# Transfers asked for beside other work in a two-block transformer kernel: stages without computation removed, tables ahead of the zeros, the residual one tile behind the sums

## The reference, cut to what matters

```python
def first_block(x, c, ctx, ...):          # two layers; layer 0 also keeps the context
    for l in range(DEPTH):
        mod = silu(c) @ w_mod[l] + b_mod[l]              # shift, scale, gate, twice
        h = x * (1 + scale) + shift
        y = mixer_ab(h) if l == 0 else mixer_na(h)       # attention (+ Fourier mixing)
        x = layer_norm(alpha * x + gate * y, ln1)        # ln1 stage
        h = x * (1 + scale) + shift                      # h2 rows, stored to DRAM
        m = moe_ffn(h)                                   # 64 experts, top 8, one shared
        x = layer_norm(alpha * x + gate * m, ln2)        # combine stage

def fourier_mix(f, w_fnet):
    fr = fft2(f over tokens and 64 channels).real        # as products with tables
    return einsum("blgc,gcd->blgd", fr, w_fnet)

def second_block(x, ...):
    for i in range(DEPTH):
        h = h + 0.5 * rms_norm(swiglu(rms_norm(h)))      # ffn
        h = h + rms_norm(mixer(rms_norm(h)))             # conv + state space, or dilated attention
        h = h + 0.5 * rms_norm(swiglu(rms_norm(h)))      # ffn
```

## Time and profile before

| | |
|---|---|
| median of 3 runs | 3317.04 us (3316.82 to 3324.07) |
| profiled execution, its own time | 3318.03 us |
| its span, first to last instruction | 3316.2 us |
| TensorE busy / VectorE / ScalarE / GpSimd | 80% / 36% / 25% / 7% of the span |
| mean granted TensorE clock | 0.893 of full |
| TensorE weight loads | 56% of the span |
| moved | 810.85 MB, 245 GB/s over the span |

### The profile page before, as it was taken

One profiled execution on the slowest core, in us unless ns is written; L12 is line 12 of the kernel. 1 busy time (PEld: TensorE's weight loads), 2 busy tenths in 40 slices (PEclk: granted clock), 3 DMA queues, 4 the chain that ended last, 5 costly groups with the idle time before them and its releaser, 6 DMA issues. The chain is left out here.

```text
span 3316.2 us, 44216 instructions
## 1 busy us (share of the span) xinstructions
PE 2650.5 (80%) x17438; PEld 1848.6 (56%) x17438; DVE 1184.3 (36%) x1841; ACT 844.0 (25%) x1237; POOL 238.3 (7%) x210
## 2 busy tenths in 40 slices
PE   5777499999997598597744537999678979989699
PEld 4656444333342475343222217987437979987598
DVE  2433442211113535311110035449515445345344
ACT  2132111111111323111100004326314344334433
POOL 0000200121004010101100020000000000000000
PEclk8888689999998799699887768999798989989899
DMA  6373679999998323799999954423044434332451
GB/s 255 162 288 146 270 309 424 412 373 411 426 370 321 124 87 145 288 400 424 410 411 425 408 209 177 176 91 143 2 190 178 177 140 190 152 137 77 175 206 70
DMA packets 120122, 810.85 MB, mean 245 GB/s; under 512 B 31752, under 2 KB 33416, under 8 KB 67848
## 3 DMA queue, kind: packets, MB, share of 16 engines
q1 hardware_dynamic: 86264, 718.88, 54.0%
q0 software_dynamic: 19168, 53.65, 4.2%
q10 hardware_dynamic: 14512, 35.89, 2.8%
HBM read 762.12 MB, written 56.84 MB: 247 GB/s over the span
## 5 line engine op out<-in xcount | busy, mean ns | idle before, releaser
L2378 PE MATMUL psum<-second_x_hi,ffn_up_hi 128*128 128x256 f32 x1408 | 402.1, 286 | 45.4 <-DVE ffn_up_lo L2453 45.4
L2378 PE MATMUL psum<-second_x_lo,ffn_up_hi 128*128 128x256 f32 x1408 | 401.5, 285 | 0.0
L2378 PE MATMUL psum<-second_x_hi,ffn_up_lo 128*128 128x256 f32 x1408 | 401.3, 285 | 0.0
L1576 PE MATMUL psum<-experts_ahead_ring_up,moe_cols 128*64 128x512 f32 x1568 | 359.0, 611 | 35.4 <-issue 35.3
L2378 PEld LDWEIGHTS psum<-second_x_hi,ffn_up_hi 128*128 128x128 f32 x1408 | 273.6, 194 | 48.3 <-DVE ffn_up_lo L2453 46.9
L1940 DVE TENSOR_TENSOR experts_gated<-experts_silu,psum 128x256 f32<-128x256 f32 (+1 forms) x93 | 34.0, 366 | 679.7 <-ACT experts_silu L1726 679.7
L2378 PEld LDWEIGHTS psum<-second_x_lo,ffn_up_hi 128*128 128x128 f32 x1408 | 273.5, 194 | 1.4
L2378 PEld LDWEIGHTS psum<-second_x_hi,ffn_up_lo 128*128 128x128 f32 x1408 | 273.4, 194 | 0.0
L1583 PE MATMUL psum<-experts_ahead_ring_up,moe_cols 128*32 128x256 f32 x2432 | 170.6, 443 | 115.6 <-issue 115.6
L1576 PEld LDWEIGHTS psum<-experts_ahead_ring_up,moe_cols 128*64 128x64 f32 x1568 | 114.7, 141 | 245.4 <-issue 244.6
L2453 DVE TENSOR_TENSOR ffn_up_lo<-second_ring_up,ffn_up_hi 128x4096 fp32r<-128x4096 f32 x44 | 194.4, 4425 | 121.2 <-ACT ffn_up_hi L2415 121.2
(11 more groups left out here) (509 smaller groups left out, 4396.5 us busy)
## 6 DMA issues: line engine op xcount, KB each, us to landing
experts_ahead_ring_up<-in_experts SPq DMA_DIRECT2D x130, 2048.0 KB, 25.4
experts_ahead_ring_down<-in_experts SPq DMA_DIRECT2D x130, 1024.0 KB, 23.0
second_ring_up<-in_ffn SPq DMA_DIRECT2D x44, 2048.0 KB, 9.2
second_ring_down<-in_ffn SPq DMA_DIRECT2D x44, 1024.0 KB, 5.0
results<-experts_y ACTq DMA_DIRECT2D x49, 512.0 KB
second_ring_up<-in_attn_w_qkv SPq DMA_DIRECT2D x9, 2048.0 KB, 7.7
results<-ab_att_zeros SPq DMA_DIRECT2D x32, 512.0 KB, 13.6
ab_ahead_ab_in_w<-in_w_mod SPq DMA_DIRECT2D x6, 2048.0 KB, 16.0
```

Of the source, the lines that this page charges most:

```text
L1576: last = nc.tensor.matmul(psum[64 * e:64 * e + 64, bank, :], x[:, k, 64 * e:64 * e + 64], w[:, k, :, :].rearrange("p a n -> p (a n)"), sta ...
L2378: last = nc.tensor.matmul(psum[:, 2 * m + kind, 0:LAT], w[:, j, k, at], h[:, k, :], start=k == 0 and which == 0, stop=k == KD - 1 and whic ...
```

## The change

- `transpose_stage` and `rms_stage` take a function of SP's requests, run beside the stage's work. The requests of `ab_out` and of the first norm vectors go beside `qk_t`, those of `RouterInputs` beside `h2_cols`, the second block's first weights beside `first_rms`, with the small gain tables now ahead of them.
- The four first experts' weights are asked for at the start of `experts_stage`, by pairs: up, up, down, down.
- The Fourier tables have tiles of their own from before the attention stage on (class `Fourier`). They are asked for at the start of the attention stage, with the wait until they have landed, and then the zeros. The wait for the zeros goes into the third Fourier stage.
- Layer 1's modulation has a fourth buffer (the keys' tile, free by then), so its fourth chunk is asked for beside the turning `na_o`; VectorE runs `beside.dve` after its second tile's factors, ahead of the gains.
- Combine: four pairs of banks instead of two, so TensorE does not wait for `added`; SP asks for the vectors when the second gather has landed, gates first; VectorE's residual of tile t comes after the sums of tile t+1.

```diff
@@ class Modulation
+        if last is not None:
+            self.slots.append(last)
         self.depth = len(self.slots)
@@ class Vectors
-    def loads(self, sp):
-        for i, v in enumerate(self.vectors):
+    def loads(self, sp, gates_first=False):
+        order = list(range(len(self.vectors)))
+        for i in order[2:] + order[:2] if gates_first else order:
@@ def residual_norm_stage
-                beside.more_loads(sp)
+                if next_loads is None:
+                    beside.more_loads(sp)
                 beside.store(sp)
...
+                if step == 1 and next_loads is not None:
+                    beside.dve(dve)
                 if step >= 2:
...
-            if beside is not None:
+            if beside is not None and next_loads is None:
                 beside.dve(dve)
@@ def attention_stage
                 if idle_fill is not None:
                     sp.wait_ge(cleared, 1)
-                    fills = idle_fill.shape[0] // P
-                    for b in range(fills):
-                        sp.dma_start(idle_fill[b * P:(b + 1) * P, :], zeros[:]).then_inc(filled, 16)
-                    sp.wait_ge(filled, 16 * fills)
+                    for b in range(idle.shape[0] // P):
+                        sp.dma_start(idle[b * P:(b + 1) * P, :], zeros[:]).then_inc(filled, 16)
@@ class Fourier
+    def loads(self, sp):
+        sp.dma_start(self.tok[:], self.dft_tokens).then_inc(self.loaded, 16)
+        sp.dma_start(self.chan[:], self.dft_channels).then_inc(self.loaded, 16)
+        sp.wait_ge(self.cleared, 1)
+        for g in range(4):
+
+            at = slice((g % 2) * 64, (g % 2) * 64 + 64)
+            sp.dma_start(self.mix[at, g // 2, at], self.w_fnet[g]).then_inc(self.loaded, 16)
+        sp.wait_ge(self.loaded, 96)
@@ def fourier_stages, third stage
+            @block.sync
+            def _(sp):
+                zeros_there(sp)
@@ class ExpertRing
-        with nc.Block() as block:
-            @block.sync
-            def _(sp):
-                for item in range(KEPT):
-                    self.load_up(sp, item, self.place(item))
-                    self.load_down(sp, item, self.place(item))
+    def kept_loads(self, sp):
+        for pair in range(KEPT // 2):
+            for item in (2 * pair, 2 * pair + 1):
+                self.load_up(sp, item, self.place(item))
+            for item in (2 * pair, 2 * pair + 1):
+                self.load_down(sp, item, self.place(item))
@@ def experts_stage
+            ring.kept_loads(sp)
             sp.wait_ge(order_known, 1)
@@ def combine_norm_stage
-            sp.wait_ge(gathered[TOP_K - 1], 16)
-            vectors.loads(sp)
+            sp.wait_ge(gathered[1], 16)
+            vectors.loads(sp, gates_first=True)
...
-                if t >= 2:
-                    pe.wait_ge(added, (t - 2) * (TOP_K - by_pe) + 1)
...
-            for t in range(n):
-                sums(t)
-                if t >= 1:
-                    factors(t - 1)
-                residual(t)
-                if t >= 1:
-                    gain(t - 1)
+            for step in range(n + 1):
+                if step < n:
+                    sums(step)
+                if step >= 2:
+                    factors(step - 2)
+                if step >= 1:
+                    residual(step - 1)
+                if step >= 2:
+                    gain(step - 2)
             factors(n - 1)
             gain(n - 1)
@@ def first_block
                 transpose_stage(nc, f"h2_cols{layer}", psum, ident, KD, tok_tiles, lambda j, t: acc[:, t, j * P:(j + 1) * P],
-                                lambda engine, j, bank: copy_on(nc, engine, cols[:, j, 0:tok_tiles * P], bank[:, 0:tok_tiles * P]))
+                                lambda engine, j, bank: copy_on(nc, engine, cols[:, j, 0:tok_tiles * P], bank[:, 0:tok_tiles * P]), inputs.loads)
...
-                vectors.start()
+
+                def qk_loads(sp):
+                    for c in range(out_stream.depth):
+                        out_stream.load(sp, c)
+                    vectors.loads(sp)
+
+                zeros, filled = st.sbuf("zeros", [P, D]), st.sem("filled")
+                fourier = Fourier(nc, st, i["ab_w_fnet"], i["dft_tokens"], i["dft_channels"])
...
-                part = modulation(st, "mod_rest2", 1, 8, 4, 1, later=stream.wbuf, later_free=True)
+                part = modulation(st, "mod_rest2", 1, 8, 4, 1, later=stream.wbuf, later_free=True, last=k[:].rearrange("p c n -> p (c n)"))
@@ def second_block
-                part_loads(0)(sp)
-                sp.dma_start(gains[:], i["norm_g_cols"]).then_inc(loaded, 16)
-                sp.dma_start(ssm_gain[:], i["ssm_norm_g_cols"]).then_inc(loaded, 16)
-                sp.wait_ge(loaded, 32)
-        rms_stage(nc, "first_rms", x, acc, D, 2, x[:, 2, :])
+        def first_loads(sp):
+            sp.dma_start(gains[:], i["norm_g_cols"]).then_inc(loaded, 16)
+            sp.dma_start(ssm_gain[:], i["ssm_norm_g_cols"]).then_inc(loaded, 16)
+            part_loads(0)(sp)
+            sp.wait_ge(loaded, 32)
+
+        rms_stage(nc, "first_rms", x, acc, D, 2, x[:, 2, :], loads=first_loads)
```

108 lines of the change are left out of this document (53 added, 55 removed).

## The result

The changed kernel runs in 3290.39 us (median of 4 runs, 3289.31 to 3291.27) against 3320.19 us (4 runs, the three shown and one more): a ratio of 0.991, with a 95% interval of 0.9893 to 0.9927. It is faster, but by half of what was forecast (3256, range 3247 to 3267). The profiled execution takes 3289.31 us, its span is 3287.1, 29.1 us less than before.

The account below looks back on a forecast made before the run. Each stage ends with its slowest engine, so stretches where the computing engines idle (request blocks, three transfer waits) are time of the span. The terms sum to 61.0 us off 3318.0, giving 3257.0, stated as 3256; range 3247 to 3267.

Parts of the forecast that it names:

- Ahead of the attention: Output weights' requests beside the turning before the attention, which starts at 169.0 instead of 172.59: 3.6 us won.
- the first line of the table: Stretch from the start to the first attention product: 3.6 us forecast, 4.6 us won.
- Zeros and tables: Attention's end to first Fourier product: fills 3.7 us later, SP ends the stage, 11.3 us won, bounds 6 to 12.2.
- The rule on the latency of HBM under load: Wait for the Fourier tables: up to 2 us later by the skill page, total 3258; the sum did without it.
- SP holds the attention stage: Rival: tables land 5 us later, fills after them, Fourier start slips as much: 3261 to 3264; chance 0.12.
- The clock: First 13 Fourier products: after a pause of 1 to 2 us, full clock, 1.8 us won, between 0 and 1.9.
- Combine, layer 0 and layer 1: VectorE's gate-vector wait replaced by a shorter one for the second tile: 1.8 us (-3 to 5) and 3.0 (0 to 5).
- Norm, layer 1: VectorE's 6.28 us wait for vectors read back mostly gone through a fourth buffer: 5.7 us won, bounds 4 to 6.3.
- Layer 0's and layer 1's router and weights: Table requests beside the turning, router earlier: 8.7 us won in layer 0, 6.8 in layer 1 (bounds 0.5 to 8.4).
- the expert layers hide it: Rival: gathers wait for all weights, 2 to 4 us more in layer 0, nothing left in layer 1: 3265; chance 0.14.
- The seam: Between the blocks: norm starts beside the weight requests, nothing waits for weights, 18.3 us won, bounds 14 to 18.5.
- The rest of the span: Stretch from the first split of ffn weights to the end, untouched by the change: 0 us forecast.

Follow-up runs that it names:

- the restored blocks: Changed kernel with the two blocks of requests ahead of the turning restored in both expert layers: 3303.36 us, ratio 0.9947 to the kernel before.
- its repeat: The changed kernel itself run once more, unaltered, in another group of runs: 3294.43 us, ratio 0.9927 to the kernel before.
- the old stage in the changed kernel: Changed kernel with the combine stage of before (VectorE's order, requests' place and order, two pairs of banks): 3284.79 us, ratio 0.9873.
- first and third groups: Variants of the changed kernel and its repeat, beside the kernel before on one chip per group (3323.24 and 3321.04 us): 3277.77 to 3303.36 us.
- second group: Kernel before (3308.57 us) with new combine alone, 3329.16, or seam alone, 3293.71; changed kernel with wait behind fills, late vectors, old order, 3252.76, or new, 3265.56.

## Why the prediction was wrong, step by step

- **Ahead of the attention**: right. From the store of the modulation rows to the turning 3.76 us instead of 7.32. The other 1.8 us of the first line of the table were won before any changed place (the same store comes at 163.46 instead of 165.27), by chance.
- **Zeros and tables**: the step that failed is "and the last is asked for at 215.86 + 3.7 = 219.6". The half of the sentence ahead of it, "so the fills land 3.7 us later", was right: by the packed traces the last fill lands at 232.8 instead of 229.3. The prediction carried over, without saying so, how far SP's requests run ahead of the landings, 13.5 us for the last one before. With the fills begun behind a wait for the tables it is 5.0 us. So SP's last request ends at 227.8, 8.2 us after what was said, and the first Fourier product came 8.1 us late; the product's distance to VectorE's last piece is 11.0 us. Even with the 34.79 us of before, SP's last request would have ended at 223.7. The start was only 1.4 us later than assumed. The rule on the latency of HBM under load (the Trainium skill, "DMA: Bandwidth & Descriptors", section "Latency and other measured facts") would have moved the start up to 2 us to the same side; but the DMA share is 0.17 from 186 to 188, so no high load is shown where the wait ends, and it is the small part. The rival "SP holds the attention stage" had the right engine and not the cause: its tables land 5 us late, they landed 1.4 us late; it was priced at 5 to 8 us where this part fell short by 12, the clock with it.
- **The clock**: rested on the step above. With a pause of 11.6 us the clock fell as before (1.0 us lost). Where the pause was 1.36 us, it was 1.00 and 1.8 us were won against the earlier trace rows, as said.
- **Combine, layer 0 and layer 1**: the steps that failed are "it waits there instead, from 1049.9 (the wait's start) to 1054.3 at least" and "The vectors asked for earlier share the DMA engines with the gathers; the sum of bytes is the same". The end of TensorE's second tile was read off the trace of a kernel in which nothing stood in front of those gathers. With the vectors in front it moved from 25.3 to 33.1 us after the first gather in layer 0, and from 25.1 to 32.0 in layer 1, where that costs 6 to 7 us. And the sum of bytes says when the last gather lands, not what VectorE can still do before it: in layer 0 the last wait is the third tile's, at 43 us, which the prediction did not look at, and the new order leaves 7 to 8 us more behind it. In the changed kernel the second tile is so late (sums at 35.6) that the third's start at 45.1 without a wait, 2 us behind 43; with the 37.3 us that the new order leaves this makes the 82.4. The bounds, -3 in layer 0 and 0 in layer 1, were not low enough (-9.5 and -4.3).
- **Norm, layer 1**: right, 5.6 for 5.7.
- **Layer 0's and layer 1's router and weights**: right in kind, 10.7 for 8.7 and 5.8 for 6.8, in part by luck. The same code gives 643.4 to 651.7 us for layer 0's stretch in the nine traces with the new place, and 647.5 to 655.0 in the four with the old one; the means are 6 us apart, in layer 1 4 us. The gathers lost 3.8 us to the weights instead of 1.6, inside the bounds; in return the experts behind them took 596.3 us instead of 599.9. The rival "the expert layers hide it" has one thing right, layer 0's gathers lose 2.2 us more than said; but that nothing is left in layer 1 is refuted by the restored blocks.
- **The seam**: right, 18.8 for 18.3. A wait that was said not to be there is: the second split waits 2.88 us for its weights. It costs nothing that the trace shows: but for the 3.3 us below, the rest of the span is as long as before.
- **The rest of the span**: 3.1 us lost in stretches without any change. 3.3 of them lie between the first ffn's last split and the second ffn's first, 319.5 before and 322.8 after. The thirteen traces show two values, 319.2 to 320.3 in eight of them and 322.8 to 323.4 in five; the changed kernel shows 322.8 in its first trace and 319.4 in its repeat. It is chance, not cost.

Together: 12 us short in the Fourier part, 11.3 and 7.3 in the combine stages, 3.1 by chance, and small ones both ways; 29.1 us won where 61.0 were forecast.

## What beats both

The changed kernel with SP's wait behind the fills, VectorE's old order, and the vectors after the eighth gather with the gates first: 0.9821 of the kernel before (0.9795 to 0.9847), against 0.991 (0.9893 to 0.9927) for the changed kernel. Of the order put down in the change one half is worth keeping, the gates ahead of gain and shift: layer 1's combine takes 42.0 us with it, the shortest of all, where it is 47.6 with gain and shift first; layer 0's stays at 73.0.

## What to carry to other kernels

A wait put ahead of a list of requests costs at least its length if the list ends the stage: here the list began 7.85 us later and ended 11.9 us later. How far requests run ahead of their landings is no constant (5 to 6 us or 13 to 15 here), so a forecast may move the landings, but not the last request with them; put the wait behind the list. In a stage bound by transfers, work belongs ahead of the last wait for them; moved behind it, it cost 7 us here. Where the last wait is, depends on the number of tiles. Before moving a transfer forward, name what it now stands in front of.

## What was not expected

- POOL's 16 requests for the same transfers took 0.54 us each to the end, while its fills landed up to 30 us later; SP's first ones took 0.35 to 0.8 us, and on average it was 1.21 where the queue was empty at the start, 1.15 and 1.09 where weights lay ahead. Why SP is held back at another distance than POOL, stays open.
- The router phase of layer 0, from its first product to the first gather, takes 26.4 to 26.9 us or 19.1 to 19.7, by the granted clock. Its first 20 us in the changed kernel and in its repeat:

```profile
376.56:396.56 20.00, 18.32 (x93) 17.99 (x93) 6.95 (x25) 2.17 (x5) 1.76 (x1) 0.53 0.96 381
```

```profile
377.89:397.89 20.00, 17.58 (x121) 17.00 (x121) 9.86 (x33) 2.18 (x5) 2.39 (x2) 0.77 0.96 375
```

  The 7 us are not won: the gathers then meet more of the weights (10.8 us to the turning instead of 8.7), and from the first table to combine's first gather it is 644.2 and 643.6 us.
- The combine stage of layer 0 shows a wait that no code explains. With the old stage in the changed kernel, TensorE's second tile ends 25.2 us after the first gather, yet VectorE, and POOL's 26th gather, start at 35.3, released by something that the profile calls "remote":

```profile
1039.52 6.17 PE L2056 MATMUL psum<-combine_rows,combine_diagonal 128*128 128x512 f32 x14
...
1055.82 1.28 DVE L2102 SCALAR_TENSOR_TENSOR block_acc<-combine_rows,moe_share,psum 128x1024 f32<-128x1024 f32 x1 [3.44 <-remote]
1055.84 0.94 POOL L2068 DMA_INDIRECT combine_rows<-results,moe_result_rows  x1 [4.31 <-remote]
```

  A late start of this kind shows in the changed kernel and in the rest of the first and third groups, whatever the order, and in no kernel of the second group. It makes 76.8 out of 73 here, and is the likely part of the changed kernel's 82.4 that is over 80. The packed traces say more. Both engines wait for the semaphore that TensorE's products raise. In the kernel before and in the second group its updates follow the products' ends by 0.02 us. Here the second tile's last three come at 35.06, 35.12 and 35.18 us (35.31 to 35.43 in the changed kernel), where the trace has these products end at 21.7 to 25.2; in the changed kernel the updates are 2 to 6 us behind. The same traces lack semaphore updates: of the 512 that layer 0's gathers make, they hold 193 to 245, where the other five hold all. Whether the updates come late or the recording of them slows the stage, was not settled; it is why layer 0's stages are best compared among those five.
